# First mixer of a two-block transformer kernel: window attention on head pairs with rounded operands, gated attention spread between projection and window

## The reference, cut to what matters

```python
qa, ka, va, qb, kb, vb, rb, zg = jnp.split(z @ w_in, split_points, axis=-1)   # of tokens, and of context
o_a = window_attention(axial_rope(qa), axial_rope(ka), va, cka, cva, sink)
o_b, oc_b = bidir_gla(qb, kb, vb, la_f, la_b, cqb, ckb, cvb, cla_f, cla_b)
y = jnp.concatenate([o_a, gla_output(o_b, rb, gla_g)], axis=-1) @ w_out

def window_attention(q, k, v, kc, vc, sink):      # 8 query heads of 64, 2 key/value heads, blocks n of 128 tokens
    s_band = where(valid, q[n] @ k[n-1:n+2].T * scale, -inf)      # valid: |kpos - qpos| <= 128
    s_ctx = q[n] @ kc.T * scale                                   # 256 context keys
    p = softmax(concat([s_band, s_ctx, sink]))
    return p[:nk] @ v[n-1:n+2] + p[nk:nk+256] @ vc

def gla_chunked(q, k, v, log_a, s0):              # 4 heads, keys of 64, values of 128, chunks of 64 tokens
    g = cumsum(log_a); q_t = q * dk**-0.5 * exp(g); k_t = k * exp(-g); k_end = k * exp(g_last - g)
    o = where(lower, q_t @ k_t.T, 0) @ v + q_t @ S            # S the state before the chunk
    S = exp(g_last) * S + k_end.T @ v                         # once forward, once backward
def gla_output(o, r, gla_g): return rmsnorm(o, gla_g) * silu(r)
```

## Time and profile before

| | |
|---|---|
| median of 3 runs | 3571.97 us (3570.65 to 3572.16) |
| the profiled execution | 3574.16 us, its span 3572.4 us |
| PE busy | 3329.2 us, 93% of the span |
| DVE, ACT, POOL busy | 1913.6, 1021.8, 28.6 us |
| PEclk, 40 slices, in tenths | `6999999995568999999997999989999969789999` |

### The profile page before, as it was taken

The page is one execution under the profiler, slowest core; times in us unless marked ns, Lnnn a source line. Parts: engine busy times, 40 slices in busy tenths (PEclk is TensorE's granted clock), DMA queues, the critical chain, the costliest instruction groups (busy, mean ns, idle before and its releaser), DMA issues.

```text
span 3572.4 us, 36382 instructions
## 1 busy us (share of the span) xinstructions
PE 3329.2 (93%) x14711; PEld 2617.8 (73%) x14722; DVE 1913.6 (54%) x2707; ACT 1021.8 (29%) x1466; POOL 28.6 (1%) x31
## 2 busy tenths in 40 slices
PE   4999999999988999999996999989999989789998
PEld 3778888786766788778884788768887745367886
DVE  6875554624235554566647554466656534454444
ACT  2221222326213222232223222232223334232222
POOL 2000000000000000000000000000000000000000
PEclk6999999995568999999997999989999969789999
DMA  4443432120002443245631444235542200023221
GB/s 180 137 135 106 136 126 77 50 67 1 1 1 83 147 148 124 89 138 192 212 119 52 136 153 136 89 102 185 191 165 79 83 25 1 0 83 100 89 95 59
DMA packets 101858, 365.17 MB, mean 102 GB/s; under 512 B 11234, under 2 KB 12514, under 8 KB 101436
## 3 DMA queue, kind: packets, MB, share of 16 engines
q1 hardware_dynamic: 97644, 351.65, 29.6%
q10 hardware_dynamic: 2944, 6.29, 0.5%
q0 software_dynamic: 1104, 4.90, 0.4%
HBM read 360.70 MB, written 2.10 MB: 102 GB/s over the span
## 4 chain that ended last, share of the span: by engine, by line
PE 88%; DVE 7%; ACT 2%; DMA 1%; issue 1%; another core or an unknown queue 0%; ACTq 0%; POOL 0%; DVEq 0%; SPq 0%
PE ps L184 23%; PE ps L186 23%; PE ps L185 23%; PE ps L188 4%; PE ps L189 2%; PE ps L1362 1%; DVE WL L176 1%; PE ps L1267 1%; PE ps L2351 1%; PE ps L1316 1%; PE ps L2415 1%; PE ps L1272 1%; DVE DUMP L297 1%; DMA STG<-in_w_modt 1%; PE ps L2147 1%
## 5 line engine op out<-in xcount | busy, mean ns | idle before, releaser
L184 PE MATMUL ps<-HH,WH 128*128 128x512 f32 x2464 | 980.4, 398 | 29.8 <-DVE HL L557 27.9
L185 PE MATMUL ps<-HL,WH 128*128 128x512 f32 x2464 | 967.9, 393 | 0.0
L186 PE MATMUL ps<-HH,WL 128*128 128x512 f32 x2464 | 967.7, 393 | 0.0
L171 ACT ACTIVATE WH<-RAW 128x1024 fp32r<-128x1024 f32 x456 | 456.8, 1047 | 571.8 <-PE ps L186 410.4
L176 DVE TENSOR_TENSOR WL<-RAW,WH 128x1024 fp32r<-128x1024 f32 x456 | 538.6, 1221 | 99.4 <-ACT WH L171 99.2
L184 PEld LDWEIGHTS ps<-HH,WH 128*128 128x128 f32 x2464 | 467.9, 190 | 137.0 <-issue 36.9
L185 PEld LDWEIGHTS ps<-HL,WH 128*128 128x128 f32 x2464 | 468.0, 190 | 101.2 <-issue 5.0
L186 PEld LDWEIGHTS ps<-HH,WL 128*128 128x128 f32 x2464 | 467.3, 190 | 100.8
L808 DVE SCALAR_TENSOR_TENSOR XT<-ps,DER,XT 128x512 f32<-128x512 f32 x512 | 342.7, 682 | 272.1 <-PE ps L186 257.9
L184 PE MATMUL ps<-GH,WH 128*128 128x512 f32 x1056 | 414.0, 392 | 19.1 <-DVE XT L808 14.3
L186 PE MATMUL ps<-GH,WL 128*128 128x512 f32 x1056 | 412.1, 390 | 0.0
(11 more groups left out here) (306 smaller groups left out, 2749.9 us busy)
## 6 DMA issues: line engine op xcount, KB each, us to landing
RAW<-in_w_modt SPq DMA_DIRECT2D x200, 512.0 KB, 4.4
RAW<-in_ffn_wi SPq DMA_DIRECT2D x176, 512.0 KB, 4.5
RAW<-in_ffn_wo SPq DMA_DIRECT2D x88, 512.0 KB, 4.6
RAW<-in_w_gu SPq DMA_DIRECT2D x88, 512.0 KB, 4.4
RAW<-in_w_in SPq DMA_DIRECT2D x44, 512.0 KB, 3.6
RAW<-in_w_down SPq DMA_DIRECT2D x44, 512.0 KB, 4.3
RAW<-in_w_out SPq DMA_DIRECT2D x16, 512.0 KB, 3.7
MU<-in_w_mod SPq DMA_DIRECT2D x8, 384.0 KB, 8.3
```

Of the source, the lines that this page charges most:

```text
L171: act.e.activation(u.hi, u.ld.view, ACT.Copy).then_inc(u.hi_done.sem, 1)
L184: pe.e.matmul(out, wh, x[0], start=first, stop=False)
L185: pe.e.matmul(out, wh, x[1], start=False, stop=False)
L186: m = pe.e.matmul(out, wl, x[0], start=False, stop=last)
```

## The change

The window attention works on pairs instead of units: both sides of a head pair go together.

- `WinScore`: Q and K are split in hi and lo (`HiLo`, on ACT and DVE), and the score is a sum of three fp32r products instead of one f32 product; the two sides stand on rows 0 to 63 and 64 to 127 of the array and write to `wide[0]` and `wide[1]`. The next pair's scores wait for both exponentials of this one.
- `WinPV`: the values (128 x 64) are stationary, P transposed is moving (128 tokens), and the two sides write to partitions 0 to 63 and 64 to 127 of one bank, already feature-major. `WinOut` goes; `WinDen` and `WinQuot` spread the reciprocal sums by a matmul with ones and multiply.
- Gated attention: gates, logarithm, scans and the first half of the end factors move into the projection (`gla_gates`, one piece after each of 10 chunks), whose chunks are reordered (queries after values). One 1536-wide logarithm per direction takes the place of four. The states' steps are 12, with the second direction one step late. `GlaAtt`, `GlaOut` and `GlaNorm` are by 128 tokens (4 blocks instead of 8 chunks), with Q stationary, on bank 7 alone, and are added between pieces of the window instead of behind it. The normalisation is by tokens: its sums are a DVE reduction, then transposes.
- `window` now yields after each of its three parts, so a piece of `gla` follows each part of a pair.
- The split of the gated half of `MIX` for the output projection and of its first weights comes inside `gla`; the output products take features 4 to 7 first. P and its transpose lie in four of the six `RAW` buffers during the window, so that weights have two buffers there.

```diff
-        pe.e.matmul(wide[:, 512 - nk:512], q, w.KA[rows, bl[0] * 128:bl[0] * 128 + nk], start=True, stop=True)
-        for o, m, there in ((512 - nk, 0, n > 0), (384, 1, n < 3)):
...
+        def product(Q, K, first):
+            for par in range(2):
+                bl, nk, wide, view = self.view(par)
+                r = slice(64 * par, 64 * par + 64)
+                pe.e.matmul(wide[:, 512 - nk:512], Q[r, j, n * 128:(n + 1) * 128], K[r, bl[0] * 128:bl[0] * 128 + nk],
+                            start=first, stop=True, skip_group_check=not first)
+            for par in range(2):
+                wide, r = w.P.wide[par], slice(64 * par, 64 * par + 64)
+                m = pe.e.matmul(wide[:, 512:768], Q[r, j, n * 128:(n + 1) * 128], K[r, T:W],
+                                start=first, stop=True, skip_group_check=not first)
+            return m
+        product(w.QH, w.KH, True)
...
+        product(w.QH, w.KL, False)
+        product(w.QL, w.KH, False).then_inc(self.scored.sem, 1)
...
+        before = w.trans.get(q - 1)
+        self.bankfree = [before.first + [before.rest] if before else [], [w.bank5free] + (before.first if before else [])]
+        self.ptfree = w.pv[q - 2].done if q > 1 else NONE
+        w.trans[q] = self
+    def tensor(self, pe):
+        w, P = self.w, self.w.P
+        for par in range(2):
+            pe.wait_ge(*self.sc.exp[par])
+            for t in self.bankfree[par]:
...
         for i, b in enumerate(bl):
-            m = pe.e.matmul(P.banks[6][:, self.hs * 64:self.hs * 64 + 64], w.PT[:, self.v % 3, i * 128:(i + 1) * 128],
...
+            for par in range(2):
+                r = slice(64 * par, 64 * par + 64)
+                m = pe.e.matmul(P.banks[6][r, j * 128:(j + 1) * 128], w.VA[:, b, r],
+                                w.PT[:, self.q % 2, par, i * 128:(i + 1) * 128], start=i == 0, stop=i == len(bl) - 1,
+                                skip_group_check=True)
...
-                         w.P.banks[4].rearrange("p (c t) -> p c t", t=128), ACT.Copy).then_inc(self.done.sem, 1)
+        pe.wait_ge(*self.bankfree)
+        for par in range(2):
+            r = slice(64 * par, 64 * par + 64)
+            pe.wait_ge(*self.den.diag[par])
+            m = pe.e.matmul(P.banks[5][r, :], P.ONE[:, 0:64], w.D[:, 2 * par:2 * par + 2, :], start=True, stop=True,
+                            skip_group_check=True)
+        m.then_inc(self.spread.sem, 1)
...
+    def tensor(self, pe):
+        g, P = self.g, self.g.P
...
-        for d in range(2):
-            c = g.seq[d][i]
+        for d, k in self.parts:
+            c = g.seq[d][k]
+            r = slice(64 * (c % 2), 64 * (c % 2) + 64)
             pe.wait_ge(*g.ken[d])
-            for p in range(2):
-                for par in range(2):
-                    r = slice(64 * par, 64 * par + 64)
-                    m = pe.e.matmul(P.banks[7][r, d * 256 + p * 128:d * 256 + (p + 1) * 128], g.KEN[d][r, c, p, :],
-                                    g.VV[r, c, p, :], start=True, stop=True)
+            for h in range(4):
+                o = slice(64 * (h % 2), 64 * (h % 2) + 64)
...
+            for odd in range(2):
+                r = slice(64 * odd, 64 * odd + 64)
+                pe.e.matmul(P.banks[7][r, h * 128:(h + 1) * 128], g.AB[r, B % 2, h * 64:h * 64 + 64],
+                            g.VV[r, B, h * 128:(h + 1) * 128], start=h == 0, stop=False, skip_group_check=True)
+        for h in range(4):
+            m = from_states(h, h % 2, True)
+        m.then_inc(self.half.sem, 1)
+        pe.wait_ge(*self.half)
+        for h in range(4):
+            m = from_states(h, 1 - h % 2, True)
         m.then_inc(self.done.sem, 1)
...
             self.units = self.split([w[0]])
-            ms = self.add(MixSplit(self, MIX, MH, ML, ready))
-            sums = Sums(self, T)
...
-                self.side_by_side(self.window(w), self.gla(gla, w))
...
+                order = [GZ, AV, AK] + list(range(GK, GR)) + [0, 1, 2, 3] + list(range(GR, GZ)) + [GQ, GQ + 1]
...
+                def beside(ch):
+                    if ch == GR - 1:
+                        g.ctxdone = self.group
+                    elif ch < AK or GQ <= ch < GK or ch >= GR and ch != AV:
+                        next(gates, None)
...
+    def window(self, w, QA):
         self.add(WinSink(w))
-        for u in range(len(w.units) + 2):
-            if u < len(w.units):
...
-                    yield
-                    self.add(WinOut(w, (u - 2) // 8))
-            yield
-        w.ended = [w.out[3].done, w.score[31].exp, w.score[30].exp]
-    def gla(self, g, w):
-        self.add(GlaMasks(g))
+        for j in range(4):
+            w.qsplit[j] = HiLo(self, QA[:, j, :], w.QH[:, j, :], w.QL[:, j, :], [])
+            self.add(w.qsplit[j])
+        last = len(w.pairs)
+        for q in range(last + 2):
+            if q < last:
+                self.add(WinScore(w, q))
+                yield
+            if 1 <= q <= last:
+                self.add(WinTrans(w, q - 1))
+                yield
+                if q % 4 == 0:
+                    self.add(WinDen(w, q // 4 - 1))
+            if q >= 2:
+                self.add(WinPV(w, q - 2))
+                if q % 4 == 1:
+                    self.add(WinQuot(w, q // 4 - 1))
+                yield
+            if 1 <= q <= last and w.trans[q - 1].nb == 5:
+                self.add(WinRest(w, q - 1))
...
+    def gla_gates(self, g, pr):
         for d in range(2):
             for p in range(2):
                 for c0, c1 in ((0, T), (T, W)):
-                    self.add(GlaGate(g, d, p, c0, c1))
-                    yield
+                    self.add(GlaGate(g, pr, d, p, c0, c1, [g.ctxdone]))
+                yield
+            self.add(GlaLog(g, d))
+            for p in range(2):
                 self.add(GlaScan(g, d, p))
+            yield
+        self.add(GlaEnd(g, 0, g.GA))
+        yield
+        self.add(GlaEndExp(g, 0))
+        yield
+        self.add(GlaKE(g, 0))
+        yield
...
+    def gla(self, g, KE, mix, w_out):
+        g.mask = self.add(PoolLoad(self, "gla_mask", [(g.MK[:, :, :], self.a["gla_mask"])])).landed
+        self.add(GlaEnd(g, 1, KE))
+        self.add(GlaEndExp(g, 1))
+        for q in range(3):
+            self.add(GlaKen(g, 0, q))
+            if q == 0:
+                self.add(GlaKE(g, 1))
+            yield
         for d in range(2):
-            self.add(GlaQ(g, d))
+            self.add(GlaDec(g, d))
+        for q in range(3):
...
-            yield
-            self.add(GlaKMul(g, d))
-            self.add(GlaEnd(g, d))
-            yield
-            self.add(GlaEndExp(g, d))
-            yield
-            self.add(GlaKE(g, d))
-            for q in range(3):
-                self.add(GlaKen(g, d, q))
-                yield
-        for i in range(11):
+        exps = iter([(GlaQ, 0), (GlaQMul, 0), (GlaK, 0), (GlaKMul, 0), (GlaQ, 1), (GlaQMul, 1), (GlaK, 1), (GlaKMul, 1)])
+        for i in range(12):
             self.add(GlaState(g, i))
             yield
-        while 3 not in w.out:
+            if i % 2:
+                for _ in range(2):
...
+                    if e:
...
-                self.add(GlaAtt(g, c + 1, w.ended))
-            self.add(GlaOut(g, c))
-        self.add(GlaNorm(g))
+            self.add(GlaOut(g, B))
+            yield
+        self.add(GlaNewton(g))
+        yield
+        for B in range(4):
+            self.add(GlaNorm(g, B))
+            yield
+        self.new_ring()
+        self.add(MixSplit(self, mix, range(4, 8), [g.done]))
+        self.units = self.split([w_out[0]])
+        yield
...
+            self.add(MixSplit(self, mix, range(4), [w.quot[3].done]))
```

854 lines of the change are left out of this document (463 added, 391 removed).

## The result

The median of 4 runs is 3448.84 us (3448.61 to 3450.88), where the kernel before took 3571.31 beside it (4 runs): ratio 0.9658, 95% interval 0.9642 to 0.9675. That is faster by 3.4%. The forecast was 3463, 14 us above the median, and its range holds the measured time. The profiled execution took 3450.88 us, its span 3449.1.

What follows compares the result with a forecast made beforehand. PE's work at the half clock was taken to bound the first mixer's attention: 277.4 us becomes 152, gaining 125.4, less 17 in the projection, 108.4 off 3574.16, less 2.2 to the median: 3463 us, range 3436 to 3517.

Steps and rivals of the forecast that it cites:

- The projection, +17: First mixer's projection: added gate products, late weight splits and a clock dip lengthen it by 17 us, between +5 and +25.
- The start: Start of the new attention stage: the fourth pair's scores start 26 us in, with PE working 13 of these.
- Work of a pair on PE: Window attention at the half clock: a pair takes 7.45 us with three neighbour blocks, 5.8 with two.
- near ends: Window products, half clock: scores 1.9 us with weight loads mostly hidden; P times V 2.4 for 20, other end 5.0.
- Rival (c): Tiles sharing the array's rows gain little in P times V, states and spread: 3485 us, chance 0.12.
- The path over DVE: Stage at the full clock: a pair with two state rounds needs 7.2 us on DVE's path against PE's 5.6.
- the tail: End of the attention stage at the full clock: 4 us of added waiting.
- The clock: Attention stage: clock rises with the states, a third of PE's later work stays at half level; 135 + 28 - 10 = 152 us.
- Rival (a): Clock stays at the half level throughout the attention stage: stage 198 us, time 3509, chance 0.24.
- fill both halves of the array: Reason given for the clock's rise: new scores and P times V use the whole array, as state rounds do.
- (d): Tiles do not run together at all in the new forms and the clock stays half: 3630 us, chance 0.05.
- (e): Edits cancel through bank waits, pairs taking some 14 us in the states: stage 250 or more, little better; chance 0.03.

## Why the prediction held, point by point

**The projection, +17.** It measured 160.1 - 143.2 = 16.9. The sum was right and its parts were not, which is partly luck. The forecast had 4 of work, 10 of stalls and 3 of clock. PE's waits there are 5.2 on L183 and 2.2 on the rope's side bank. With the split two chunks ahead 7.5 came back, which shows the cause of those, and 9.4 above the kernel before are left where the forecast had 4.

**The start.** The forecast had 26 us until the fourth pair's scores; they start at 838.44, 21 us after 817.39. That is five too many.

**Work of a pair on PE.** Scores and masks were put at 1.9 + 0.65 = 2.55 at the half clock; in the run with P stationary, whose scores are the same, they take 869.79 - 867.06 = 2.73 there. P times V was put at 2.4 for 20; at 939.90 it takes 2.16 at the half clock, 1.24 at the full. Both near ends were right. Rival (c) is refuted by the run with the columns apart: sharing rows, two tiles still gain 1.57 times. The Trainium skill, "TensorE: Matmul & The Clock Gate", Part 3, "What overlaps and what doesn't", lets a weight load overlap a running matmul only where the row group differs. This trace disagrees with it: at 869.46 all tiles stand on the same 128 rows, and PEld is busy with its 20 loads for 1.07 of the 1.24 us in which PE works.

**The path over DVE.** The forecast had 7.2 us for a pair with two rounds; 7.5 and 7.1 were measured (871.07, 878.56, 885.62 are starts of scores). PE waited 7.3 us on L1800 where 9 were put down, 2.1 in the attention blocks where 7 were, 8.0 at the norms where the tail had 4.

**The clock: the step that was mis-sized.** I took a third of PE's later work at the half level, and wrote 135 + 28 - 10 = 152 (it is 153). The window from the fourth pair's scores to the end of the stage shows what came:

```profile
838.44:958.87 120.43, 97.66 (x1127) 74.85 (x1126) 69.92 (x160) 54.22 (x110) 0.00 (x0) 0.91 0.01 3
```

A granted clock of 0.91 means that about 22 of these 120 us were at the half level (an estimate: 0.18 of 120.43), where a third of 168 us, 56, was forecast. They lie at 857 to 864, behind a wait of 2.77 us on L1800, and between 925 and 942, among waits of 3.48, 1.99 and 2.49 us on L1948. So PE's work was 98 us where 112 were put down (84 + 28), its waits 23 us where 15 were (25 - 10), and the start 21 where 26 were. Two errors were too high and one too low, so that the stage missed by 10.5 us only (141.5 against 152). Rival (a), the half clock throughout, is refuted.

**Behind the stage.** The other 4.2 us of the miss lie there: from the first output product to the end 2490.2 us passed, 2494.4 before (3572.4 - 1077.99). The forecast let nothing follow from the clock there. The old output projection began at the half clock (0.56 in its first 5 us, its first product 0.77 long at 1077.99), the new one at the full (1.00, 0.50 long). That fits the 2.0 us which it and what follows up to the next norm's products save (48.06 before, 46.10 now); the other 2.2 were not located.

**Why the clock rose: right outcome, wrong reason.** The prediction expected the rise because the new products "fill both halves of the array", and "once the states begin". The time is refuted by the changed kernel itself: the clock was full at 836.24, 3.5 us ahead of the first state round. Pairs alone had a full clock as well, and states alone did not raise it. The filled array was not needed in P times V nor in most of the scores, since with both issued side after side the clock is 0.98. The argument against rival (a), twice the array in use, therefore did not hold, and that the clock rose all the same owes something to luck.

What the runs show instead is which products go with the half level. Over 840 to 950 the granted clock is 0.81 with P stationary and 0.61 with all of the old products, against 0.89 to 0.98 in all runs with the values stationary and the gated rounds between the pairs. This is not a rule for the form: with P stationary the clock was full in the kernel before from 1000 to 1020. Which property of the form does it is open. P stationary is also twice as wide in its stationary part, half as long in its moving part, and cannot put two tiles side by side, and no run varied one of these alone.

The Trainium skill, "TensorE: Matmul & The Clock Gate", Part 4, does not count transposes as PE-busy for the clock. Here too the rise came with transposes: PE ran only these from 832.73 to 836.24, behind the scores of a pair. As scores stand just before, that neither supports nor refutes it.

**Rivals (d) and (e)** are excluded by the overlap (2.49 against 1.61) and by the pair's 7.5 us.

## What to carry to other kernels

When a stretch stands at the half clock with PE busy throughout, try the other choice of the stationary operand before counting instructions: here a swap of the operands of P times V was worth 27 us by the medians (16 by the profiled executions), side-by-side tiles 14, and fp32r in place of f32 scores 3.5. Try the order too, since it was worth more than the products: 68 of the 122 us stayed with all of the old products, and taking turns between window and gated attention was worth 55. Work hidden beside a dense stage must leave the next split of weights ahead of it in every queue it uses; count the queue positions on ACT as well as on DVE. A step moved "to where it is needed" costs what its first engine's queue holds there (10 to 18 us, where a gain of 1 was forecast).

## What the runs showed of the hardware

- Two column halves on the same rows, f32, at the full clock: 0.062 us an instruction in turn, 0.097 on one half in a row. Weight loads were busy for 1.07 of these 1.24 us.
- In the changed kernel the clock fell after PE had waited: behind 2.77 us ending at 857.47, and behind 3.48 us ending at 924.50, then 0.50 to 0.68 in most of the stretch until 940. With the scaling ahead, where the longest wait there is 1.9 us, it stayed at 1.00. With P stationary it also fell at 852 and 896, behind waits of 1.1 us that left the changed kernel at 1.00, and stayed at 0.50 with PE busy for 10.00 of 10 us.
- Over 840 to 950 PEclk was 0.91 in the changed kernel and with the rows apart, 0.97 with the columns apart, 0.98 with both, and 0.98 with the scaling ahead. PE's busy time does not order these (89.9, 93.6, 91.6, 94.6, 89.3 us), and no run separates why.
- With P stationary the time scattered over 26 us from run to run, with all of the old products over 22, with the query parts as needed over 9; the other new kernels stayed within 5. The kernel before, which has P stationary too, took 3570 to 3575 us in most runs and near 3590 in 3 of 11, with a granted clock of 0.908 to 0.910 over the whole kernel, against 0.913 to 0.916.
